# Inversions: both directions' products of a half level issued together, the neighbouring groups' pieces behind them; the last weight unit ordered by token tile

## What is computed

```python
for layer in range(DEPTH):
    h = rms_norm(x, norm_mix[layer])
    x = x + (even_mixer(h, ...) if layer % 2 == 0 else odd_mixer(h, ...))
    x = x + memory_cross_attention(rms_norm(x, ...), rms_norm(mem, ...), ...)
    x = x + squared_relu_mlp(rms_norm(x, norm_ffn[layer]), ffn_w1[layer], ffn_w2[layer])
...
# delta rule, each chunk, head and direction
    a_mat = jnp.where(strict, jnp.einsum('bnhid,bnhjd->bnhij', kb, kc) * decay, 0.0)
    unit_lower = a_mat + jnp.eye(C, dtype=a_mat.dtype)
    u = solve(unit_lower, vb)
    w = solve(unit_lower, kb * jnp.exp(gc)[..., None])
...
# RWKV-7, each token
    sa = jnp.einsum('bhij,bhj->bhi', state, a_t)
    state = state * w_t[:, :, None, :] + sa[..., None] * b_t[:, :, None, :] + v_t[..., None] * k_t[:, :, None, :]
```

## Time and profile before

| | |
|---|---|
| Time, median of 3 runs | 2749.48 us (2747.58 to 2749.55) |
| The profiled execution's own time | 2747.25 us |
| Its span, first to last instruction | 2745.4 us |
| PE busy in the span | 2708.8 us (99%) |
| DVE, ACT, POOL busy | 1539.4, 1307.1, 119.8 us |
| Chain that ended last, by engine | PE 94%, DVE 3%, ACT 2%, issue 1% |
| Delta rule's inversions, in the span | about 361 to 465 us |
| RWKV's inversions, in the span | about 1740 to 1868 us |

### The profile page before, as it was taken

One profiled execution on the slowest core, in us unless ns is written; L12 is line 12 of the kernel. 1 busy time (PEld: TensorE's weight loads), 2 busy tenths in 40 slices (PEclk: granted clock), 3 DMA queues, 4 the chain that ended last, 5 costly groups with the idle time before them and its releaser, 6 DMA issues.

```text
span 2745.4 us, 43738 instructions
## 1 busy us (share of the span) xinstructions
PE 2708.8 (99%) x18000; PEld 2367.9 (86%) x18000; DVE 1539.4 (56%) x2048; ACT 1307.1 (48%) x1794; POOL 119.8 (4%) x167
## 2 busy tenths in 40 slices
PE   8999999999999999999999999999999999999999
PEld 7999998888888888888898997787888888888887
DVE  5655466666555555545544665756665555555554
ACT  4544444555544534445444344334565444354453
POOL 0000043000000000000000000440000000000000
PEclk9999999999999999999999999999999999999999
DMA  7554411544555555555555563004445555555553
GB/s 278 181 184 169 174 43 41 206 171 151 184 200 184 186 197 184 192 191 184 188 180 193 196 217 112 17 2 148 175 148 189 187 182 199 190 188 189 191 192 138
DMA packets 67786, 461.46 MB, mean 168 GB/s; under 512 B 7023, under 2 KB 10223, under 8 KB 13084
## 3 DMA queue, kind: packets, MB, share of 16 engines
q1 hardware_dynamic: 63824, 449.47, 45.9%
q10 hardware_dynamic: 3500, 5.21, 0.6%
q0 software_dynamic: 288, 4.19, 0.4%
HBM read 456.73 MB, written 5.27 MB: 168 GB/s over the span
## 4 chain that ended last, share of the span: by engine, by line
PE 94%; DVE 3%; ACT 2%; issue 1%; DMA 0%; POOL 0%; DVEq 0%; ACTq 0%; POOLq 0%
PE bank L428 40%; PE bank L452 17%; PE bank L454 9%; PE bank L475 6%; PE bank L477 6%; PE bank L476 6%; PE bank L1225 1%; PE bank L1198 1%; PE bank L590 1%; PE bank L2613 0%; DVE split_lo L367 0%; PE bank L534 0%; PE bank L347 0%; PE bank L2165 0%; PE bank L2108 0%
## 5 line engine op out<-in xcount | busy, mean ns | idle before, releaser
L367 DVE TENSOR_TENSOR split_lo<-raw,split_hi 128x1024 fp32r<-128x1024 f32 x836 | 1014.4, 1224 | 926.3 <-ACT split_hi L360 925.8
L360 ACT ACTIVATE split_hi<-raw 128x1024 fp32r<-128x1024 f32 x836 | 876.8, 1059 | 1119.5 <-PE bank L428 546.4
L452 PE MATMUL bank<-hT,split_hi 128*128 128x512 f32 x2048 | 723.1, 398 | 0.0
L454 PE MATMUL bank<-hT,split_lo 128*128 128x256 f32 x2048 | 574.9, 281 | 0.0
L452 PEld LDWEIGHTS bank<-hT,split_hi 128*128 128x128 f32 x2048 | 384.6, 188 | 95.1 <-DVE hT L623 0.6
L428 PE MATMUL bank<-split_hi,u_hi 128*128 128x512 f32 x1152 | 449.8, 390 | 0.0
L428 PE MATMUL bank<-split_hi,u_lo 128*128 128x512 f32 x1152 | 448.4, 389 | 0.0
L428 PE MATMUL bank<-split_lo,u_hi 128*128 128x512 f32 x1152 | 448.4, 389 | 0.0
L454 PEld LDWEIGHTS bank<-hT,split_lo 128*128 128x128 f32 x2048 | 386.9, 189 | 0.2
L475 PE MATMUL bank<-hT,split_hi 128*128 128x256 f32 x1328 | 376.8, 284 | 0.0
L476 PE MATMUL bank<-hT,split_hi 128*128 128x256 f32 x1328 | 375.8, 283 | 0.0
(11 more groups left out here) (470 smaller groups left out, 2119.0 us busy)
## 6 DMA issues: line engine op xcount, KB each, us to landing
raw<-in_stream SPq DMA_DIRECT2D x420, 1024.0 KB, 4.8
work<-in_mem POOLq DMA_DIRECT2D x2, 2048.0 KB, 7.9
bias_rows<-bias_line SPq DMA_DIRECT2D x1, 3072.0 KB, 13.8
x<-in_x SPq DMA_DIRECT2D x1, 2048.0 KB, 9.2
out<-x SPq DMA_DIRECT2D x4, 512.0 KB, 4.9
mwork<-bias_rows ACTq DMA_DIRECT2D x1, 1536.0 KB, 9.8
work<-bias_rows ACTq DMA_DIRECT2D x1, 1536.0 KB, 10.0
rwork<-in_wide ACTq DMA_DIRECT2D x1, 1280.0 KB, 6.1
```

The source lines that it names most:

```text
L360: nc.scalar.activation(split_hi[:, u % SPLIT], raw[:, b % RAW, (u % 2) * UNIT:(u % 2 + 1) * UNIT], ACT.Copy).then_inc(s_hi, counted(u))
L367: nc.vector.tensor_tensor(split_lo[:, u % SPLIT], raw[:, b % RAW, (u % 2) * UNIT:(u % 2 + 1) * UNIT], f32(split_hi[:, u % SPLIT]), SUB).th ...
L452: nc.tensor.matmul(out[:, :], lhsT=w_hi[:, cols], rhs=hT[:, k].rearrange("p two s -> p (two s)"), start=k == 0, stop=False)
L454: m = nc.tensor.matmul(out[:, S:2 * S], lhsT=w_lo[:, cols], rhs=hT_hi[:, k, :], start=False, stop=k == KD - 1)
```

## The change

Two edits. In `pe_inv_level` the calls of `between` move: the half level's two products now follow each other on TensorE, and the pieces of both slots come behind the second, in the order of the slots. The pieces, the waits of each and the queues of ACT, DVE and POOL stay as they are.

```diff
@@ pe_inv_level, first half @@
                         i = nc.tensor.matmul(aux[d][right, m * HALF:(m + 1) * HALF], lhsT=AT[d][left, m, right],
                                              rhs=T[left, d, m, :], start=True, stop=True)
                 i.then_inc(iv_p, 1)
+            for d in range(2):
                 between(4 * level - 4 + d)
             for d in range(2):
                 pe.wait_ge(iv_ps, iv_p_of(group, level, d))
@@ second half @@
                     i.then_inc(iv_q, 1)
-                    between(4 * level - 2 + d)
                     continue
...
                 i.then_inc(iv_q, 1)
+            for d in range(2):
                 between(4 * level - 2 + d)
```

```diff
+                    if by_token and k >= k_tiles - 2:
+                        k, t = k_tiles - 2 + n // 3 % 2, (n - 3 * NT * (k_tiles - 2)) // 6
...
+                    if by_token and (k, t, j) == (k_tiles - 1, 0, 2):
+                        m.then_inc(s_end, 1)
...
-            for c in range(4):
+            for c in range(3):
                 wait_chunks_taken(sp, n_chunks - 3 + c)
...
-            sp.wait_ge(s_out, 4 * 16)
+            g = n_chunks - 1
+            for t in range(NT):
+                sp.wait_ge(s_taken[g % 2], g // 2 * 2 + t + 1)
+                sp.dma_start(x_out[t * P:(t + 1) * P, 3 * 512:], x[:, t, 3 * 512:]).then_inc(s_out, 16)
+            sp.wait_ge(s_out, 5 * 16)
...
                     for t in range(NT):
+                        if halved and t == 0:
+                            dve.wait_ge(s_end, 1)
+                        elif halved:
+                            dve.wait_ge(s_used, turn * FF_UNITS + chunk_done(name, c))
```

More of the change, by code:

```diff
@@ L268, in build @@
         s_out = sem("s_out")
+        s_end = sem("s_end")
         iv_mt = [sem("iv_mt0"), sem("iv_mt1")]
@@ L413, in row_unit, with row_part @@
                 return units_before(self.name, c) + u
-            def row_part(self, c, lhsT, first, last, k_tiles=KD, k_ready=None, after_unit=None):
+            def row_part(self, c, lhsT, first, last, k_tiles=KD, k_ready=None, after_unit=None, by_token=False):
                 g = self.chunk0 + c
@@ L433, in row_part, with row_chunk @@
                             after_unit(k // 2)
-            def row_chunk(self, c, lhsT, k_tiles=KD, k_ready=None, after_unit=None):
-                self.row_part(c, lhsT, 0, k_tiles * NT * 3, k_tiles, k_ready, after_unit)
+            def row_chunk(self, c, lhsT, k_tiles=KD, k_ready=None, after_unit=None, by_token=False):
+                self.row_part(c, lhsT, 0, k_tiles * NT * 3, k_tiles, k_ready, after_unit, by_token)
             def wide_chunk(self, c, k_ready=None):
@@ L1035, in one_turn @@
                 for c in range(4, 8):
-                    mlp.row_chunk(c, u_tile, k_ready=u_ready if c == 4 else None, after_unit=lambda u, c=c: turn_x(c, u))
+                    mlp.row_chunk(c, u_tile, k_ready=u_ready if c == 4 else None, after_unit=lambda u, c=c: turn_x(c, u),
+                                  by_token=(l, turn, c) == (1, FF_TURNS - 1, 7))
             for turn in range(FF_TURNS):
@@ L1131, in one_turn @@
                     banks, taken = chunk_banks(name, c)
-                    dve.wait_ge(s_used, turn * FF_UNITS + chunk_done(name, c))
+                    halved = last and (l, c) == (1, 7)
+                    if not halved:
+                        dve.wait_ge(s_used, turn * FF_UNITS + chunk_done(name, c))
                     for t in range(NT):
+                        if halved and t == 0:
+                            dve.wait_ge(s_end, 1)
+                        elif halved:
+                            dve.wait_ge(s_used, turn * FF_UNITS + chunk_done(name, c))
                         cols = x[:, t, (c - 4) * 512:(c - 3) * 512]
```

## The result

The change makes the kernel slower: 2778.44 us, the median of 6 runs (2768.77 to 2782.62), against 2748.74 us for the kernel before (6 runs, 2747.02 to 2751.0). The ratio is 1.0105, 95% interval 1.0093 to 1.0118. The forecast was slower by 14.5 us, to 2764, with a range up to 2773. The sign was right, the size was not: the change costs 29.7 us, twice the forecast, and the time lies outside the range.

A forecast was written before the change was run, and what follows sets the result against it. TensorE's queue was taken as the bound, with level 1's P(1) released by DVE's transpose. The terms 12.15 - 0.8 + 2.0 + 1.2 - 0.4 - 1.7 + 3.2 - 1.0 gave +14.65, or 14.5 us: 2764, range 2755 to 2773.

The forecast's parts named there:

- What bounds the kernel: TensorE is busy 99% of the span; in level 1, P(1) starts only when DVE's transpose releases it.
- the first two rivals: Saved tile-shape trips and DVE's earlier turn: faster, 2744, chance 0.05; losses taken up again later: no difference, 2749, chance 0.08.
- Level 1: In seven groups, pieces that ran while P(1) waited for DVE come behind P(1): 12.15 us more in all.
- Level 6: Fill moves behind P(1), baring its wait: -0.8 us in delta rule, +2.0 in RWKV, +0.9 and +0.3 in last groups.
- The other levels and the end: Saved trips -0.4 us, DVE's earlier turn in hp 1 and hp 2 -1.7, f 1 to f 3 +3.2, end -1.0.
- a rival with a chance of 0.17: Added idle time in levels 1 and 6 drops TensorE's clock; four more slow stretches cost 8 us more: 2772, chance 0.17.

The follow-up runs named there:

- the waits filled: The changed kernel with additional products that nobody reads put between P(0) and P(1) of level 6 and, except in the first group, level 1: 2761.79 us.
- levels 1 and 6 put back: The changed kernel with the first half's pieces of levels 1 and 6 each behind their own product again, as before the change: 2746.60 us.
- only the first halves moved: The kernel before with only the first halves' products, P(0) and P(1), together and their pieces behind them; second halves and end as before: 2770.77 us.

## Why the prediction was wrong, point by point

**What bounds the kernel: right.** TensorE's queue, and P(1) of level 1 released by DVE's transpose. P(1) of hp 2 in after stands behind 1.46 us of idle time, ended by that transpose. (In before, P(1) followed not the transpose but the pieces in f 0 and f 2, by 1742.70 - 1742.45 = 0.25 and 1810.35 - 1808.80 = 1.55 us, so not all seven groups show this wait. The sum allowed for it in f 2, not in f 0.) With that the first two rivals fall: P(1) was not ready when P(0) ended, and nothing later took the loss up again, since the kernel with the waits filled ends 14.8 us later.

**Level 1: right in each group looked at.** The kernel with the waits filled shows the order at before's clock. In hp 3, P(1) to Q(0) took 444.66 - 442.96 = 1.70 us in before (its Q(0) is the first row here, its P(1) in the earlier trace rows) and takes 447.86 - 444.31 = 3.55 with the waits filled: +1.85, forecast 1.85. The bracket of the row between shows the wait for ACT's copy of step 0, 0.69, which the prediction put at 0.85. In RWKV, from P(0) of level 1 to P(0) of level 2, f 0 takes 1752.17 - 1744.50 = 7.67 us against 1746.21 - 1740.16 = 6.05: +1.6, forecast 1.8. In f 2 it is 8.02 against 6.52, +1.5, forecast 1.5; in f 3 7.04 against 5.02, +2.0, forecast 1.9. The granted clock is 1.00 in all six stretches. Before, then waits filled, for hp 3:

```profile
444.66 1.12 PE L1225 MATMUL bank<-work,hwork 64*64 64x32 f32 x32
```
```profile
444.31 0.68 PE L1214 MATMUL bank<-hwork,work 64*64 64x64 f32 x16 [0.37 <-DVE hwork L1285]
...
446.77 1.16 PE L1589 MATMUL bank<-hwork 128*128 128x128 f32 x8 [0.69 <-ACT hwork L1783]
447.86 1.12 PE L1243 MATMUL bank<-work,hwork 64*64 64x32 f32 x32
```

**Level 6: right where it was looked at.** In the delta rule the way from level 6 to the next P(1) of level 1 gets shorter by 0.24 us (hp 0: from the row at 377.80 to 385.38 in before, from 378.69 to 386.03 with the waits filled), forecast 0.27. For f 3 the sum had +0.3, since P(1) waited for DVE in any case. The fill that covered part of that wait now stands behind P(1), but there it covers another one: in before, Q(1) stood behind 0.74 us of idle time until ACT's copy. From P(1) to the first product behind level 6 it took 1867.76 - 1865.27 = 2.49 us, and takes 1883.76 - 1881.18 = 2.58: +0.1. The rows are those of before, then with the waits filled:

```profile
1865.27 0.67 PE L1203 MATMUL bank<-work,hwork 64*64 64x64 f32 x8 [0.51 <-DVE work L1284]
1865.79 0.63 PE L1212 MATMUL bank<-work 64*64 64x64 f32 x8
1867.15 0.67 PE L1212 MATMUL bank<-work 64*64 64x64 f32 x8 [0.74 <-ACT work L1247]
1867.76 1.98 PE L2548 MATMUL bank<-raw,mem_kT 128*128 128x512 f32 x4
```
```profile
1881.18 0.68 PE L1219 MATMUL bank<-work,hwork 64*64 64x64 f32 x8 [0.73 <-DVE work L1303]
1881.78 1.16 PE L348 MATMUL bank<-const 128*128 128x128 f32 x8
...
1883.76 1.98 PE L2587 MATMUL bank<-raw,mem_kT 128*128 128x512 f32 x4
```

**The other levels and the end: right.** With levels 1 and 6 put back their parts are -2.1, +2.6 and -1.1, forecast -2.1, +3.2 and -1.0. In after the bare wait ahead of tail step 4 in f 1 to f 3 is 0.47 us each, forecast 0.6; one row stands for all three:

```profile
1797.59 1.10 PE L2683 MATMUL bank<-work,rwork 128*128 128x64 f32 x8 [0.47 <-ACT work L2782]
```

**The step that failed: the clock entered the sum with nothing.** The prediction saw the mechanism in the earlier trace rows, a clock of 0.59 behind a stretch with 1.2 us of idle time, and it worked out that the change lays bare 0.8 us in each level 6 and 1.2 to 1.7 us in each level 1. But it made no term of it. It kept it as a rival with a chance of 0.17, and priced that rival at 8 us for four more stretches. What the runs show is 29.7 - 14.8 = 14.9 us, half of the whole cost. In the profiled execution, the shortest of the six, it is less: its span is 2766.9 - 2758.6 = 8.3 us above that with the waits filled, about the price of the rival. So the rival came near to the mildest execution, and the forecast without it near to none. Two readings led there. The fill at slot 20 was taken for a cover of DVE's wait, worth 0.8 us, while leaving it out costs 6.6 us. And the rival was held against RWKV's few existing falls, not against the number of new idle times: eight in level 6 and seven in level 1. Not each of them brings the clock down, but each can.

**The range was too narrow for the same reason.** Its upper end, 2773, was about the rival's own time, 2772. The loss differs from one execution to the next: the six runs of after lie between 2768.77 us, at a mean clock of 0.994, and 2782.62, at 0.988, and the lower the clock, the longer the run. 0.006 of 2767 us is 16.6 us of full clock, of which the two times show 13.9.

## What to carry to other kernels

Where TensorE is the bound, idle time on it has two prices: its own length, and what the following work loses at the lower clock; here the second was as large as all the rest of the change. So before moving a piece out of a wait, look in the windows for a stretch with a comparable wait and its granted clock behind it, and make that a term of the sum for every wait that is laid bare, as an upper bound, since not every one brings a fall. Products that nobody reads are not always waste: see what stands behind them before they are moved or removed, and put them into a wait that can't be shortened.

## What the runs showed of the hardware

The clock can fall behind less than 1 us of idle time, and doesn't do so every time. In the kernel without the fill it fell behind 0.85 us ahead of P(1). But the kernel with only the first halves moved has a wait of the same kind at the same place, and there the clock stayed at 1.00:

```profile
375.00:385.00 10.00, 7.79 (x158) 7.03 (x155) 7.70 (x24) 5.28 (x14) 3.77 (x6) 1.00 0.01 3
```

Its TensorE was idle for 2.21 of these 10 us. After, which has the same first halves, was idle for 0.76 of them, at a clock of 0.83. The idle time makes a fall possible; which wait does it in a given execution was not settled by these runs. With the clock the time differs too: the times of after spread over 13.9 us, where those of before spread over 4.0.

"TensorE: Matmul & The Clock Gate" of the Trainium skill, in its section on a second failure mode of the clock, describes a kernel whose TensorE idles briefly and often between groups of matmuls, and whose clock goes back and forth between the two levels. The traces here agree: waits of 0.76 to 1.63 us, and clocks of 0.52 to 0.57 behind them.
